# A three-layer mixer on one Trainium2 core: later growth operands in the delta rule, no barrier ahead of mLSTM, and its gates made with the low-rank gate

## What is computed

```python
a_mat = where(strict, (k @ k.T) * beta * decay, 0) + eye        # unit lower triangular
u, w  = solve(a_mat, [v * beta, k * (beta * exp(gam))])
q_dec = q * exp(gam);  k_dec = k * exp(gam[-1] - gam)            # the "growth operands"
v_new = u - w @ S
o     = q_dec @ S + where(causal, (q @ k.T) * decay, 0) @ v_new
S     = S * exp(gam[-1]) + k_dec.T @ v_new
```

```python
proj = h @ w_in + b_in
# columns: hg_q hg_f hg_i hg_z | gla_q gla_k gla_v gla_a(16) gla_z | ml_q ml_k ml_v ml_i(4) ml_f(4) ml_o ml_z
log_alpha = log_sigmoid(gla_a @ w_a2 + b_a2) / 16                # GLA's low-rank gate
i_pre, log_f = ml_i, log_sigmoid(ml_f)                           # mLSTM's gates, 4 heads each
y = concat(norm_gate(hgrn2), norm_gate(gla), norm_gate(mlstm)) @ w_out
```

## Time and profile before

| | us |
|---|---|
| median of three runs | 3994.99 |
| lowest and highest | 3992.59, 3997.42 |
| the profiled execution, its own time | 3996.76 |
| its span, first to last instruction | 3995.0 |
| PE busy | 3836.1 |
| DVE busy | 1816.0 |
| ACT busy | 796.1 |
| POOL busy | 592.4 |
| mean granted TensorE clock | 0.983 |

### The profile page before, as it was taken

How to read it: one execution, slowest core, us unless ns; L and a number is a source line. 1 busy time by engine, 2 the same in 40 slices (tenths; PEclk the granted TensorE clock), 3 DMA queues, 4 the chain that set the end, 5 groups by cost and what they waited for, 6 DMA issues and landing times.

```text
span 3995.0 us, 32255 instructions
## 1 busy us (share of the span) xinstructions
PE 3836.1 (96%) x12831; PEld 1955.9 (49%) x12831; DVE 1816.0 (45%) x2613; ACT 796.1 (20%) x977; POOL 592.4 (15%) x630
## 2 busy tenths in 40 slices
PE   8999999999899899989999999999899999899998
PEld 4555444544346776454444444444356554544554
DVE  8576434435655542255633232324645553424432
ACT  2112111111452211351310000000323320221121
POOL 0343210122112220132122222222000000000000
PEclk9998999999999999999999999999999999999999
DMA  5332121111011110200111111111101001012101
GB/s 143 82 72 81 42 64 33 42 42 42 22 42 43 27 43 16 74 22 17 58 42 42 42 42 42 42 43 44 38 19 38 24 9 48 14 32 84 32 11 53
DMA packets 291233, 175.01 MB, mean 44 GB/s; under 512 B 24103, under 2 KB 281998, under 8 KB 290830
## 3 DMA queue, kind: packets, MB, share of 16 engines
q1 hardware_dynamic: 264736, 132.24, 12.2%
q0 software_dynamic: 9424, 22.30, 2.1%
q10 hardware_dynamic: 16926, 18.43, 1.4%
HBM read 159.72 MB, written 13.21 MB: 43 GB/s over the span
## 4 chain that ended last, share of the span: by engine, by line
PE 87%; DVE 8%; ACT 2%; issue 1%; POOL 1%; DMA 0%; ACTq 0%; DVEq 0%; POOLq 0%
PE products L359 39%; PE products L161 10%; PE products L3336 8%; PE products L3349 3%; PE products L2523 3%; PE products L1735 3%; DVE work L1446 2%; PE others L3415 2%; PE products L2532 1%; PE products L179 1%; PE others L2398 1%; PE others L2411 1%; PE others L1877 1%; ACT work L214 1%; PE others L2719 1%
## 5 line engine op out<-in xcount | busy, mean ns | idle before, releaser
L359 PE MATMUL products<-gate,s_small 128*128 128x512 f32 x752 | 334.6, 592 | 0.0
L3336 PE MATMUL products<-normed,weights 128*128 128x512 f32 (+2 forms) x704 | 314.8, 596 | 3.7 <-DVE normed L845 3.7
L161 PE MATMUL products<-normed,weights 128*128 128x512 f32 x704 | 309.1, 599 | 8.8 <-DVE s_small L4080 4.0
L359 PE MATMUL products<-work,s_small 128*128 128x512 f32 x640 | 289.1, 596 | 3.3 <-DVE residual L427 2.2
L377 POOL TENSOR_TENSOR s_small<-weights 128x512 f32<-128x512 f32 x66 | 86.6, 1312 | 1268.1 <-PE products L359 1128.1
L359 PE MATMUL products<-normed,s_small 128*128 128x512 f32 x512 | 232.0, 596 | 3.2 <-DVE row L415 2.2
L359 PEld LDWEIGHTS products<-gate,s_small 128*128 128x128 f32 x752 | 142.9, 190 | 179.8 <-issue 179.8
L161 PEld LDWEIGHTS products<-normed,weights 128*128 128x128 f32 x704 | 133.9, 192 | 176.4 <-issue 164.9
L214 ACT ACTIVATE s_small<-products 128x512 f32<-128x512 f32 (+1 forms) x72 | 44.6, 621 | 847.9 <-PE products L359 825.7
L359 PE MATMUL products<-normed,weights 128*128 128x512 f32 x448 | 203.9, 598 | 3.0 <-ACT normed L214 3.0
L3336 PEld LDWEIGHTS products<-normed,weights 128*128 128x128 f32 (+2 forms) x704 | 123.7, 182 | 158.4 <-issue 156.6
(11 more groups left out here) (516 smaller groups left out, 5937.8 us busy)
## 6 DMA issues: line engine op xcount, KB each, us to landing
weights<-in_w_in_dram SPq DMA_DIRECT2D x83, 512.0 KB, 3.9
weights<-in_w_up_dram SPq DMA_DIRECT2D x32, 512.0 KB, 4.8
weights<-in_w_down_dram SPq DMA_DIRECT2D x32, 512.0 KB, 4.6
weights<-in_sgu_w_in_dram SPq DMA_DIRECT2D x24, 512.0 KB, 5.1
weights<-in_s_w_in_dram SPq DMA_DIRECT2D x16, 512.0 KB, 4.7
weights<-in_w_out_dram SPq DMA_DIRECT2D x24, 256.0 KB, 2.8
branch_scratch<-work POOLq DMA_DIRECT2D x8, 512.0 KB, 2.9
work<-branch_scratch POOLq DMA_DIRECT2D x64, 64.0 KB, 2.6
```

The costliest lines, as they stand in the source:

```text
L161: last = pe.matmul(out[0:cols, half * BANK:(half + 1) * BANK], slot(c, b, kt, cols)[:, k, :], acts[n][:, half * BANK:(half + 1) * BANK], s ...
L359: last = pe.matmul(bank, w[:, k * P:(k + 1) * P], moving[k], start=(k == 0 and n in (1, 3, 5)), stop=(k == KT // 2 - 1), skip_group_check= ...
L3336: last = pe.matmul(out[0:cols, half * BANK:(half + 1) * BANK], slot(c, f.b, kt, cols)[:, kk, :], acts[kk][:, half * BANK:(half + 1) * BANK ...
```

## The change

Three parts. In `gdn_phase`, DVE calls `grow` after the first T and R of an iteration instead of before; PE issues the iteration's first quota of filler between `products` and `turn` instead of after `turn`; and these first quotas are 0, 3, 7, 6 quanta for the four iterations instead of 0, 0, 8, 8.

In the decay and mLSTM phases, the barrier is gone. mLSTM's first projection (`raw`, 0) is issued first, and the two last sums stand inside it, after three and six of its eight stationary blocks; PE then waits for the last reads of the PSUM banks and turns the gates; ACT waits for the last head's output before it loads the values' bias.

mLSTM's gates are no product of their own any more. The block of the fill `a` gets 32 columns: 16 of the low-rank gate, and 16 from `ml_i` on (the four `ml_i`, the four `ml_f`, and eight that nobody reads), by two loads on SP. One ACT operation with one bias column of 32 rows reads both. The block of the separate product is gone, and with it the three unread blocks.

```diff
@@ gdn_phase
-        quota += [0 if few else 8, 2] + [1 if few else 2] * (LEVELS - 1) + [...]
+        quota += [(0, 3, 7, 6)[it], 2] + [1 if few else 2] * (LEVELS - 1) + [...]
@@ tensor
             if it:
                 products(2 * it + 1)
+            advance()
+            if it:
                 turn(2 * it + 1)
-            advance()
@@ vector
         weigh(0), weigh(1)
-        grow(0), grow(1)
         for it in range(IT):
...
+            grow(2 * it), grow(2 * it + 1)
             for l in range(1, LEVELS):
...
                 weigh(2 * it + 3)
-                grow(2 * it + 2), grow(2 * it + 3)
@@ rows3_phase, loads
-        act.dma_start(c.v3["a_bias"], t["b_in_3"][0, SEG["gla_a"]:SEG["gla_a"] + 16]...)
+        for n, name in enumerate(("gla_a", "ml_i")):
+            act.dma_start(c.v3["a_bias"][16 * n:16 * n + 16, :], t["b_in_3"][0, SEG[name]:SEG[name] + 16]...)
@@ decay_phase
-    add("a", 4, 0, [(w[:, SEG["gla_a"]:SEG["gla_a"] + 16], KT, 16)], 16)
+    add("a", 4, 0, [(gates, KT, 32)], 16)
-    add("ml", U - 1, 0, [(w[:, SEG["ml_i"]:SEG["ml_i"] + 8], KT, 8)], 16)
+    c.decay_last_read = [(c.decay_read[j % 2], j // 2 + 1) for j in (n_items - 2, n_items - 1)]
+            if f.what == "a":
+                pe.wait_ge(c.vectors_loaded, 16 * (len(VECTORS) + 1))
-        work = columns_product(ml_gates, x, KT, 8)
-        for h in range(per(U - 1)):
-            advance(ml_gates.quanta // per(U - 1))
+        def last_sums(h):
             normalise(U - 1, h)
+        c.decay_last_sums = last_sums
@@ mlstm_phase
-        act.dma_start(ml.bias, t["b_in_3"][0, SEG["ml_i"]:SEG["ml_i"] + 8].partition_broadcast(P))...
+        act.wait_ge(c.decay_y, norms)
+        first = start_group(c, pe, g["raw", 0])
+        block_ready(c, pe, blk["raw", 0])
+        for k in range(KT):
+            for half in range(HALVES):
+                last = pe.matmul(first[:, half * BANK:(half + 1) * BANK], slot(c, blk["raw", 0], KT, P)[:, k, :],
+                                 x[k][:, half * BANK:(half + 1) * BANK], start=(k == 0), stop=(k == KT - 1))
+            if k in (2, 5):
+                c.decay_last_sums(k // 3)
+        last.then_inc(c.group_done, 1)
         taken(c, pe, c.ml_gates_group)
+        for last_read in c.decay_last_read:
+            pe.wait_ge(*last_read)
         for i in range(TT):
-            last = pe.transpose(c.pb[:, 1, i * 8:(i + 1) * 8], ...)
+            last = pe.transpose(c.pb[:, 1, i * 32:(i + 1) * 32], ...)
-        dve.wait_ge(c.params_loaded, loaded("ml"))
-        tt(ml.x, raw, ml.bias.unsqueeze(2).broadcast_to([P, 8, TT]), ALU.add, c.ml_x)
+        ch.done(dve.tensor_copy(ml.x, raw), c.ml_x)
+                if n == 0:
+                    dve.wait_ge(c.params_loaded, loaded("ml"))
                 value(n)
@@ build
-        then(decay_phase(c, t, norm.normed), meet=True)
+        then(decay_phase(c, t, norm.normed))
+                if len(src.shape) == 3:
+                    sp.dma_start(wide[:, :, 0:16], src[:, 0, :]...).then_inc(c.block_loaded[n % RING], 16)
+                    sp.dma_start(wide[:, :, 16:32], src[:, 1, :]...).then_inc(c.vectors_loaded, 16)
```

More of the change, by code:

```diff
@@ L52, in col @@
     return ap.broadcast_to([ap.shape[0], n])
-LOADS = (("sgu", 4), ("gdn", 7), ("fox", 2), ("ple", 1), ("rows3", 18), ("decay", 3), ("ml", 2), ("ml_rows", 2), ("final", 1))
+LOADS = (("sgu", 4), ("gdn", 7), ("fox", 2), ("ple", 1), ("rows3", 19), ("decay", 3), ("ml", 1), ("ml_rows", 2), ("final", 1))
 def loaded(name):
@@ L2211, in gdn_phase @@
         few = it < 2
-        quota += [0 if few else 8, 2] + [1 if few else 2] * (LEVELS - 1) + [3 if it == 2 and n < 2 else 2 for n in range(6)]
+        quota += [(0, 3, 7, 6)[it], 2] + [1 if few else 2] * (LEVELS - 1) + [3 if it == 2 and n < 2 else 2 for n in range(6)]
     finished = [[] for _ in quota]
@@ L3081, in rows3_phase @@
     c.v3["keep"] = c.s5b[:, 3072 + at + 12:3072 + at + 16]
-    c.v3["a_bias"] = c.s5b[0:16, 3072 + at + 16:3072 + at + 17]
+    c.v3["a_bias"] = c.s5b[0:32, 3072 + at + 16:3072 + at + 17]
     lb = c.v3["lb"]
@@ L3246, in decay_phase @@
     product("f", 3)
-    add("a", 4, 0, [(w[:, SEG["gla_a"]:SEG["gla_a"] + 16], KT, 16)], 16)
+    apart = SEG["ml_i"] - SEG["gla_a"]
+    left = w.shape[1] - 2 * apart
+    gates = w[:, left:].rearrange("r (h x) -> r h x", h=2)[:, :, SEG["gla_a"] - left:SEG["gla_a"] - left + 16]
+    add("a", 4, 0, [(gates, KT, 32)], 16)
     product("q", 3), product("z", 2, 2)
@@ L3255, in decay_phase @@
     window(5, spread(32, 12))
-    add("ml", U - 1, 0, [(w[:, SEG["ml_i"]:SEG["ml_i"] + 8], KT, 8)], 16)
     fill = {(f.what, f.u, f.n): f for f in fills}
-    ml_gates = fills.pop()
-    c.ml_gates_group, c.ml_gates_rows = ml_gates.g, E[1][0:8, :]
+    c.ml_gates_group, c.ml_gates_rows = fill["a", 4, 0].g, a_in[0:32, :]
     at, left = 0, [f.quanta for f in fills[2:]]
@@ L3379, in projections @@
                 else:
-                    yield from columns_product(f, x, KT, 16 if f.what == "a" else P)
+                    yield from columns_product(f, x, KT, 32 if f.what == "a" else P)
         work = projections()
@@ L3500, in take @@
                 taken(c, act, fill["v", 0, TT - 2].g)
-                act.activation(a_in[0:16, :], take_group(c, act, f.g)[0:16, :], ACT.Identity, bias=c.v3["a_bias"]).then_inc(read, 1)
+                act.activation(a_in[0:32, :], take_group(c, act, f.g)[0:32, :], ACT.Identity, bias=c.v3["a_bias"]).then_inc(read, 1)
             elif f.what == "z":
@@ L3562, in scalar @@
             square(U - 1, h)
-            if h == per(U - 1) - 1:
-                act.activation(c.ml_gates_rows, take_group(c, act, ml_gates.g)[0:8, :], ACT.Copy)\
-                   .then_inc(c.group_read[ml_gates.g % 2], 1)
             root(U - 1, h)
@@ L3797, in loads @@
     def loads(act):
-        act.dma_start(ml.bias, t["b_in_3"][0, SEG["ml_i"]:SEG["ml_i"] + 8].partition_broadcast(P)).then_inc(c.params_loaded, 16)
+        act.wait_ge(c.decay_y, norms)
         act.dma_start(v_bias, t["b_in_3"][0, SEG["ml_v"]:SEG["ml_v"] + BANK].partition_broadcast(P)).then_inc(c.params_loaded, 16)
@@ L3802, in tensor @@
         x = [c.B[:, kk, :] for kk in range(KT)]
+        first = start_group(c, pe, g["raw", 0])
[7 more added lines that the diff above has]
+        last.then_inc(c.group_done, 1)
         taken(c, pe, c.ml_gates_group)
+        for last_read in c.decay_last_read:
+            pe.wait_ge(*last_read)
         for i in range(TT):
-            last = pe.transpose(c.pb[:, 1, i * 8:(i + 1) * 8], c.ml_gates_rows[:, i * P:(i + 1) * P], c.ident[0:8, 0:8])
+            last = pe.transpose(c.pb[:, 1, i * 32:(i + 1) * 32], c.ml_gates_rows[:, i * P:(i + 1) * P], c.ident[0:32, 0:32])
         last.then_inc(c.ml_gates, 1)
         for what, n in order:
+            if (what, n) == ("raw", 0):
+                continue
             if what == "raw":
@@ L4002, in vector @@
         dve.wait_ge(c.ml_gates, 1)
-        dve.wait_ge(c.params_loaded, loaded("ml"))
-        raw = c.pb[:, 1, 0:64].rearrange("p (n q) -> p q n", q=8)
-        tt(ml.x, raw, ml.bias.unsqueeze(2).broadcast_to([P, 8, TT]), ALU.add, c.ml_x)
+        raw = c.pb[:, 1, 0:256].rearrange("p (n q) -> p q n", q=32)[:, 16:24, :]
+        ch.wait()
+        ch.done(dve.tensor_copy(ml.x, raw), c.ml_x)
         dve.wait_ge(c.act_step, c.act_at["ml_log"])
@@ L4421, in _ @@
                         sp.wait_ge(c.group_done, last + 1)
+                if len(src.shape) == 3:
+                    wide = slot(c, n, kt, cols)
+                    sp.dma_start(wide[:, :, 0:16], src[:, 0, :].rearrange("(k p) n -> p k n", p=P)).then_inc(c.block_loaded[n % RING], 16)
+                    sp.dma_start(wide[:, :, 16:32], src[:, 1, :].rearrange("(k p) n -> p k n", p=P)).then_inc(c.vectors_loaded, 16)
+                    continue
                 sp.dma_start(slot(c, n, kt, cols), src.rearrange("(k p) n -> p k n", p=P))\
```

4 lines of the change are left out of this document (2 added, 2 removed).

## The result

The changed kernel takes 3951.8 us, the median of four runs (3950.64 to 3953.8), against 3996.2 (3992.59 to 3997.83) for four runs of the kernel before beside them: a ratio of 0.989 [0.9878, 0.9902], 1.1% faster. The forecast was 3957.5 with a range down to 3953. So the direction, and most of the size, was as predicted, and the time fell 1.2 us under the range. Two of all runs of this document, one of the kernel before (13771.76 us) and one of *no_barrier* (6733.41), were far slower, at a granted clock of 0.39 and 0.55, and are left out of every figure.

What follows compares the result with a forecast made beforehand. PE, busy 96% of the span, was taken to bound the kernel. Third block 20.4 us plus delta rule 17.1 made 37.5 off 3995.0, forecasting 3957.5 us, range 3953 to 3968.

Steps and rivals of the forecast that it cites:

- gates' product, 32 records: End of decay: PE's separate product for mLSTM's gates goes and the wider fill costs nothing; 13.9 us gained.
- idle time at the barrier: End of decay: PE's standstill before mLSTM goes if the new order's cover suffices; 5.07 us, booked as 5.1.
- restart at 1.2 GHz: Start of mLSTM: PE's slow stretch after the idle time goes; 1.6 us gained.
- transposes, 8 records: mLSTM's gates: transposes of 32 columns instead of 8 still take 1.02 us, so 0 added.
- iteration one: Delta rule: mask at 1251.9 instead of 1254.81, level's end at 1260.0 instead of 1264.05; 4.1 us gained.
- iteration two: Delta rule: earlier masks give 3.3 us, three moved quanta 2.6, less 0.5 for the clock; 5.4 us gained.
- iterations three and four: Delta rule: filler covers the wait ahead of `turn` and keeps the clock up; 3.8 us gained each.
- rival of a short cover: End of decay: late ACT work leaves PE standing 2.3 us with a slow restart (1.9); 3961.7 us, chance 0.10.
- given back in mLSTM: mLSTM: a load or DVE sets the pace, so only the product's 13.9 us stays; 3964 us, chance 0.08.
- collision rival: Delta rule: `grow` meets POOL's masks and the clock still falls; gain 9.7 us, total 3965, chance 0.17.
- signs that were to speak against the forecast: Prediction wrong if PE waits for `kd`, masks stretch over 1.7 us, or mLSTM shows a new wait before the values.
- slower rival: Delta rule: more short gaps keep TensorE at 1.2 GHz through the solves; about 4043 us, chance 0.02.

Runs made afterwards that it cites:

- no_barrier: The kernel before with only the barrier gone, gates keeping their product and mLSTM's first projection ahead of the transposes: 3988.7 us, ratio 0.9985.
- fold_barrier: The changed kernel with the barrier kept and both last sums ahead of mLSTM's first projection: 3971.91 us, ratio 0.9946.
- experiment 2: Overwritten matmuls added ahead of mLSTM's first output-projection group: three to the kernel before, 3994.06 us; one to the changed kernel, 3958.43 us.
- masks_first: The changed kernel with POOL's two vb products moved from ahead of level one's masks to level three: 3951.92 us, ratio 0.9892.
- after_pad1: The changed kernel with one overwritten 512-column matmul added ahead of mLSTM's first output-projection group: 3958.43 us, ratio 0.9908.

## Why the prediction was nearly right, and what it missed

The total by its own terms, against the traces:

```
                                          forecast  measured
gates' product, 32 records                   13.9      13.9   (32 instructions fewer on PE)
idle time at the barrier                      5.1       5.07
restart at 1.2 GHz                            1.6       1.6
transposes, 8 records                         0         0.4   (1.02 -> 0.68)
change of stream                             -0.2       0
                         third block         20.4      21.4   (0.4 in the rest of the stretch)
iteration one                                 4.1       4.9   (from `turn` on)
iteration two                                 5.4       5.2   (5.9, less 0.5 for the clock)
iterations three and four                     7.6       7.8
                         delta rule          17.1      17.9   (18.7 by the stretch; 17.7 by
                                                               the means of five traces)
tail, untouched                               0         4.1
```

**The step that failed** is the one that is not in the sum: it was made only over stretches that the change touches, and took all others as fixed. The tail was not: put at 0, it gave 4.1 us, 3.7 of them to the end of the span. Without these the median would be some 3955.5, inside the range. In every trace here the slow stretch ahead of the end either is there (10 us) or is not (6 to 7 us, 7.7 in *fold_barrier*), and experiment 2 shows that 0.9 us of PE work elsewhere can decide it. That the change took the slow stretch away was luck: nothing in it aims there. The range could have known: the kernel before has places with a granted clock of about 0.5 behind short gaps, each worth some us either way, and the lower end of 3953 held no such term. With it the range would have begun near 3949. Its other end does not follow from its own bounds either: 9 and 16 us of gain are 3970, not 3968. Beside the tail, 2.0 us of the traces' difference lie in unchanged stretches that vary by up to 2.3 us between traces of one kernel; they are not explained further.

**Third block.** The cover was calculated to 0.3 us at each of its three places, and the rival of a short cover is out. So is "given back in mLSTM": PE waits for nothing new there. The wider block cost nothing, as worked out: the 32 records of the fill `a` take 14.4 us of busy time before and 14.5 after. The transposes were put at 1.02 us from rows 8, where they ran directly behind idle time; at the full clock they take 0.68. A row taken behind a gap carries the low clock with it.

**Delta rule, iteration one.** The step had R waiting for the whole pair `vb` and the mask for R. The timelines of DVE and POOL show it otherwise:

```profile
1247.04 0.79 DVE L2485 TENSOR_TENSOR work<-ident,work 128x512 f32<-128x512 f32 x1
...
1248.35 0.93 DVE L2485 TENSOR_TENSOR work<-ident,work 128x512 f32<-128x512 f32 x1
1249.20 1.75 DVE L2470 TENSOR_TENSOR s_small<-normed,work 128x512 f32<-128x512 f32 x1
```
```profile
1245.78 2.96 POOL L2322 TENSOR_TENSOR s_small<-gate,gate_cols 128x512 f32<-128x512 f32 x2
1248.70 6.29 POOL L2328 TENSOR_TENSOR work<-work,levels 128x512 f32<-128x512 f32 x4
```

The first R takes its turn between the two `vb` (the first ends at 1247.29, R at 1247.83), the second right behind the pair (1248.74, 1249.28). Both are there before a mask could have used them, and the mask starts at the end of `vb` (1248.70), held by POOL's own list. The second R is 2.0 us earlier than forecast (1250.5 against 1252.5 in the times of the kernel before, where `turn` starts 1.19 later), since it is no longer behind the first mask, and the second product is 1.0 us earlier; that is the 0.8 us. masks_first confirms what the mask waits for: with `vb` out of the way it starts at 1247.83, behind R.

**Iterations three and four** came out to 0.1 us each, the 0.3 of qg ahead of the second mask (0.80 to 1.11) with them.

**Iteration two** has nearly the right number because two errors cancel, so that part is luck. It was worked out at 5.9 us, and 0.5 taken off for the chance that the clock falls. The second product began 1.0 us earlier than the forecast had its mask (1326.76 against 1327.75 in the times of the kernel before), for the same reason as in iteration one. Then the clock did fall, at 1321.24 for 3.4 us: the product, the quantum and the update that start at 1320.69, 1322.08 and 1323.78 take 4.40 us, where the same three take 2.75 at the full clock. In *after_pad1* and *fold_barrier*, with the same code, the clock stays up there and iteration two gives 6.6 us.

**The rivals.** The collision rival at its price (9.7 us for the delta rule instead of 17.1) is out. Two of the signs that were to speak against the forecast did show, but small: PE waited about 0.2 us once for `kd`, since `grow` takes 6.6 us in iteration one, and masks stretched from 1.27 to as much as 1.71 us. The slower rival is out as well: from the first `k k^T` to the last state step the granted clock was low for 6.8 us after the change, and for 20.5 before.

## What to carry to other kernels

A piece of work taken out of a stream may be the cover of something else. Find what waits behind it before its time is booked as gain, and move new cover there in the same edit: the parts of the change to the third block gave 3.1 and 7.1 us, together 21.4. A wait that passes from list to list (PE to DVE to POOL) is shortened only at the list that ends it; filling PE's gap ahead of it makes the next gap longer. And where TensorE's clock falls behind short gaps, give the forecast a term of some us of either sign for such places anywhere downstream, and compare small changes by the stretch and not by the whole time. Take several traces for it: a stretch with one and the same code moved by up to 3.1 us here.

## What the runs showed of the hardware

DVE and POOL take turns by instruction. The Trainium skill (SBUF — State Buffer, Who interferes with whom) has a VectorE operation with two SBUF inputs and a GpSimd one that reads SBUF contend for a shared port, which is locked for a whole instruction. The traces agree, and show what it does to a series. A DVE operation of this kind ends 0.54 to 0.6 us after the POOL instruction it met, whenever it was issued: qg lasts 1.75 us behind a mask that ends near 1250.4, R of the second chunk 1.44 in iteration three, and either 0.68 alone. POOL does not keep the port for its next instruction: its masks last 1.27 us alone and up to 1.71 with such a neighbour. A copy of 128 x 4 elements takes 0.16 us alone and 1.23 beside the masks, while `kd` and T, which read one operand from PSUM, keep their 0.67 to 0.69. In the forecast the lock was applied to the pair `vb` as if it were one instruction.

The granted clock behind the same gap of 2.45 us, with the same work around it, was 0.54, or 0.92 to 0.93, over the tail, the same in both traces of either kernel, and changed sides when 0.9 or 2.6 us of matmuls were added some 380 us earlier. Which it was went with an offset of half a microsecond between the clock's changes and PE's work, already there 245 us ahead of the tail. What in the chip sets this offset was not measured.
